# Six lower levels of the recurrent heads as products of 32 by 32 tokens in four column groups

## The reference, cut to what matters

```python
b = cumsum(logf)                                   # per channel, over the tokens
attn[t, s] = sum_k q[t, k] * k[s, k] * exp(b[t, k] - b[s, k])   for s <= t
o[t] = sum_s attn[t, s] * i[s]     # the state between chunks is the same sum over older tokens
```

## Time and profile before

| | |
|---|---|
| median of 3 runs | 1509.45 us (1509.22 to 1509.79) |
| profiled execution, first to last instruction | 1508.1 us |
| TensorE (PE) busy | 1497.7 us, 99% |
| VectorE (DVE) busy | 970.6 us, 64% |
| ScalarE (ACT) busy | 672.4 us, 45% |
| GpSimd (POOL) busy | 99.8 us, 7% |
| levels 0 to 7 of the recurrent heads | 739.2 to 823.8 us of the span |

### The profile page before, as it was taken

How to read it: one execution, slowest core, us unless ns; L and a number is a source line. 1 busy time by engine, 2 the same in 40 slices (tenths; PEclk the granted TensorE clock), 3 DMA queues, 4 the chain that set the end, 5 groups by cost and what they waited for, 6 DMA issues and landing times.

```text
span 1508.1 us, 18663 instructions
## 1 busy us (share of the span) xinstructions
PE 1497.7 (99%) x7478; PEld 1207.1 (80%) x7478; DVE 970.6 (64%) x1250; ACT 672.4 (45%) x964; POOL 99.8 (7%) x66
## 2 busy tenths in 40 slices
PE   9999999999999999999999999999999999999998
PEld 5888888778888877778888877788888888888887
DVE  5869899997895888854478367735554444432435
ACT  4656667754543667654212445522433222222232
POOL 0000001011300000023000000000210000000110
PEclk9999999999999999999999999999999999999999
DMA  9344353434684323123212342122223232322223
GB/s 392 120 154 156 115 193 122 142 112 168 221 299 178 112 87 95 53 75 114 84 57 85 102 151 84 57 84 88 108 84 112 84 112 85 112 98 84 98 98 126
DMA packets 49311, 184.70 MB, mean 122 GB/s; under 512 B 3988, under 2 KB 21012, under 8 KB 33096
## 3 DMA queue, kind: packets, MB, share of 16 engines
q1 hardware_dynamic: 32400, 174.91, 32.4%
q10 hardware_dynamic: 16824, 8.58, 2.4%
HBM read 174.98 MB, written 4.30 MB: 119 GB/s over the span
## 4 chain that ended last, share of the span: by engine, by line
PE 95%; DVE 2%; ACT 2%; issue 0%; DMA 0%; ACTq 0%; DVEq 0%
PE bank L755 25%; PE bank L757 25%; PE bank L756 25%; PE zz L1139 1%; PE bank L1094 1%; PE tt L1071 1%; PE bank L1014 1%; PE bank L1016 1%; PE bank L1015 1%; PE tt L909 1%; PE zz L1236 1%; PE zz L1082 1%; PE tt L878 1%; PE bank L1249 1%; PE zz L1083 1%; PE zz L1174 1%
## 5 line engine op out<-in xcount | busy, mean ns | idle before, releaser
L755 PE MATMUL bank<-HH,whi 128*128 128x512 f32 x1336 | 539.2, 404 | 0.4 <-DVE HL L1347 0.4
L757 PE MATMUL bank<-HH,wlo 128*128 128x512 f32 x1336 | 521.9, 391 | 0.0
L756 PE MATMUL bank<-HL,whi 128*128 128x512 f32 x1336 | 520.9, 390 | 0.0
L1395 DVE TENSOR_TENSOR wlo<-raw,whi 128x2048 fp32r<-128x2048 f32 (+1 forms) x129 | 262.8, 2039 | 91.1 <-ACT whi L2213 82.3
L755 PEld LDWEIGHTS bank<-HH,whi 128*128 128x128 f32 x1336 | 251.1, 188 | 61.7 <-issue 11.6
L757 PEld LDWEIGHTS bank<-HH,wlo 128*128 128x128 f32 x1336 | 250.8, 188 | 54.0
L756 PEld LDWEIGHTS bank<-HL,whi 128*128 128x128 f32 x1336 | 251.4, 188 | 48.9 <-issue 2.6
L2213 ACT ACTIVATE whi<-raw 128x2048 fp32r<-128x2048 f32 (+1 forms) x107 | 202.3, 1891 | 143.3 <-PE bank L757 116.9
L2885 POOL TENSOR_TENSOR SRT<-SRT 128x512 f32<-128x512 f32 x47 | 84.5, 1797 | 899.5 <-ACT SRT L2247 897.8
L757 PE MATMUL bank<-FH,wlo 128*128 128x512 f32 x176 | 68.5, 389 | 0.0
L756 PE MATMUL bank<-FL,whi 128*128 128x512 f32 x176 | 68.5, 389 | 0.0
(11 more groups left out here) (378 smaller groups left out, 2180.1 us busy)
## 6 DMA issues: line engine op xcount, KB each, us to landing
raw<-wstream SPq DMA_DIRECT2D x113, 1024.0 KB, 4.9
aslot<-tstream SPq DMA_DIRECT2D x24, 512.0 KB, 3.4
AD<-tstream SPq DMA_DIRECT2D x24, 512.0 KB, 5.5
A<-astream SPq DMA_DIRECT2D x8, 1024.0 KB, 17.9
AC<-scratch ACTq DMA_DIRECT2D x16, 512.0 KB, 5.2
QD<-QD SPq DMA_DIRECT2D x16, 256.0 KB, 3.8
raw<-wstream SPq DMA_DIRECT2D x4, 768.0 KB, 4.2
X<-xT SPq DMA_DIRECT2D x2, 1024.0 KB, 6.8
```

The costliest lines, as they stand in the source:

```text
L755: e.matmul(o, wh[:, k, c], hi[:, kb0 + k, :], start=first and k == 0, stop=False)
L756: e.matmul(o, wh[:, k, c], lo[:, kb0 + k, :], start=False, stop=False)
L757: x = e.matmul(o, wl[:, k, c], hi[:, kb0 + k, :], start=False, stop=last and k == kb - 1)
L1395: x = e.tensor_tensor(wlo[:, i % 2, c], raw[:, i % 2, c], whi[:, i % 2, c].bitcast(F32), ALU.subtract)
```

## The change

Levels 0 to 5 lie wholly inside blocks of 32 tokens, and only these blocks of the product are now made. A level is one spell: 64 matmuls of 32 by 32 tokens (4 blocks of 128, 4 heads, 4 offsets), with the output partitions, and so the column group of TensorE's array, moving with the offset from one matmul to the next. All of a level's scores fill one bank of 128 partitions by 16 groups of 32 columns. VectorE takes them with one `copy_predicated` for a level into `AD32`, which lies in the place of `OFF[0]`; level 0 has a mask of its own in the place of the product with the identity. In each level VectorE now does both halves of `grow` first and the copy after, and TensorE's spell waits for half 1 of the level before. After level 5 ScalarE writes the packed blocks to their places in `AD` with four copies of 32 partitions. `AD` and `AD32` are set to zero by GpSimd before, once the attention of the first block is done. The masks get smaller. The yields of each engine stay the same in number: 36 for the six levels on TensorE and VectorE, 48 before the first `OFF` copy on ScalarE. Counts of `s_ad` and `s_hgl` change with the number of spells.

```diff
--- before.py
+++ after.py
@@ -305,10 +305,12 @@
     HI = sbt("HI", [128, 4, 512], F32, ph2)
     GG = sbt("GG", [128, 4, S], F32, ph2)
     AD = sbt("AD", [128, 4, 4, 128], F32, ph2)
-    mk = sbt("mk", [128, 7, 128], U8, ph2)
+    mk = sbt("mk", [128, 6, 32], U8, ph2)
     OFF = [sbt("OFF", [128, 4, 128], F32, ph2)] + [
         b[:, 512 * k:512 * k + 512].rearrange("p (h t) -> p h t", h=4)
         for b, k in ((HT[0], 0), (HT[0], 1), (HT[0], 2), (HT[0], 3), (HT[1], 1))]
+    AD32 = OFF[0][:, :, :].rearrange("p h (u t) -> p (h u) t", t=32)
+    AD_all = AD[:, :, :, :].rearrange("p b h t -> p (b h) t")
     ph2.close()
     ph2 = ExitStack()
     OB = sbt("OB", [128, 2, 4, S], F32R, ph2)
@@ -1128,23 +1130,23 @@
             run(block("hf", n, "in2"))
 
         def hgrn():
-            for x in range(24):
-                lv, cs = x // 4, slice(128 * (x % 4), 128 * (x % 4) + 128)
+            for lv in range(6):
                 w.wait_ge(s_hq, 4)
                 w.wait_ge(s_hk, 4)
                 w.wait_ge(s_rr, SUM_AT["so"])
-                w.wait_ge(s_grow, grown(lv - 1, x % 4 // 2))
-                w.wait_ge(s_ad, x - 1)
-                for h in range(4):
-                    m = e.matmul(aux[x % 2][:, 128 * h:128 * h + 128], HK[:, h, cs], HQ[:, h, cs], start=True, stop=True)
+                w.wait_ge(s_grow, grown(lv - 1, 1))
+                w.wait_ge(s_ad, lv - 1)
+                for u in range(16):
+                    tb, h = divmod(u, 4)
+                    for o in (0, 32, 64, 96):
+                        ts = slice(128 * tb + o, 128 * tb + o + 32)
+                        m = e.matmul(aux[lv % 2][o:o + 32, 32 * u:32 * u + 32], HK[:, h, ts], HQ[:, h, ts], start=True, stop=True)
                 m.then_inc(s_hgl, 1)
-                yield
-                if x % 2:
-                    yield
+                yield from idle(6)
             yield
             for lv in (6, 7):
                 w.wait_ge(s_grow, grown(lv - 1, 1))
-                w.wait_ge(s_ad, 24 if lv == 6 else 26)
+                w.wait_ge(s_ad, 6 if lv == 6 else 8)
                 for tb in range(4):
                     for h in range(4):
                         for s0, t0, t1 in LEVEL_PARTS[lv]:
@@ -1157,7 +1159,7 @@
                 if f == 2:
                     yield
                 w.wait_ge(s_grow, grown(7, 1) if f < 2 else grown(8, 1))
-                w.wait_ge(s_ad, 28)
+                w.wait_ge(s_ad, 10)
                 w.wait_ge(s_off, f - 1)
                 for h in range(4):
                     m = e.matmul(aux[f % 2][:, 128 * h:128 * h + 128], HK[:, h, 128 * s:128 * s + 128],
@@ -1905,27 +1907,24 @@
                                     ALU.mult))
 
         def hgrn():
-            for x in range(24):
-                lv, tb = divmod(x, 4)
-                bv = quads(aux[x % 2][:, :])
-                w.wait_ge(s_hgl, x + 1)
-                if lv == 0:
-                    e.tensor_tensor(AD[:, tb, :, :], bv, ident.unsqueeze(1).to_broadcast([128, 4, 128]),
-                                    ALU.mult).then_inc(s_ad, 1)
-                else:
-                    w.wait_ge(s_ad, x - 3)
-                    w.wait_ge(l_mk, 16)
-                    e.copy_predicated(AD[:, tb, :, :], mk[:, lv - 1, :].unsqueeze(1).to_broadcast([128, 4, 128]),
-                                      bv).then_inc(s_ad, 1)
-                yield
-                if tb % 2:
-                    grow(lv, tb // 2)
-                    yield
+            for lv in range(6):
+                yield
+                w.wait_ge(s_hgl, lv + 1)
+                grow(lv, 0)
+                yield
+                grow(lv, 1)
+                yield
+                w.wait_ge(s_zero, 4)
+                w.wait_ge(s_ad, lv)
+                w.wait_ge(l_mk, 16)
+                e.copy_predicated(AD32, mk[:, lv, :].unsqueeze(1).to_broadcast([128, 16, 32]),
+                                  aux[lv % 2][:, :].rearrange("p (u t) -> p u t", t=32)).then_inc(s_ad, 1)
+                yield from idle(3)
             for lv in (6, 7):
                 yield from idle(1 if lv == 6 else 3)
                 for half in range(2):
-                    w.wait_ge(s_hgl, 25 if lv == 6 else 26)
-                    w.wait_ge(s_ad, 22 + 2 * half if lv == 6 else 25 + half)
+                    w.wait_ge(s_hgl, lv + 1)
+                    w.wait_ge(s_ad, 6 if lv == 6 else 7 + half)
                     for s0, t0, t1 in LEVEL_PARTS[lv]:
                         both_tb = quads(aux[half][:, :])[s0:t0, :, s0:t1].rearrange("p h (two m) -> p two h m", two=2)
                         m = e.tensor_copy(AD[s0:t0, 2 * half:2 * half + 2, :, t0:t1], both_tb)
@@ -2660,7 +2659,13 @@
             e.activation(fs, fs, ACT.Sigmoid).then_inc(s_hs, 1)
 
         def hgrn():
-            yield from idle(48)
+            yield from idle(40)
+            w.wait_ge(s_zero, 4)
+            w.wait_ge(s_ad, 6)
+            for o in (0, 32, 64, 96):
+                x = e.activation(AD_all[o:o + 32, :, o:o + 32], AD32[o:o + 32, :, :], ACT.Copy)
+            own(x)
+            yield from idle(8)
             for f in range(6):
                 if f == 2:
                     yield
@@ -2917,6 +2922,9 @@
         run(chunks)
         run(chain(out_proj(2), out_proj(3)))
 
+        w.wait_ge(s_av, 8)
+        e.memset(AD[:, :, :, :], 0.0).then_inc(s_zero, 1)
+        e.memset(OFF[0][:, :, :], 0.0).then_inc(s_zero, 1)
         for n in range(1, 8):
             for m, acc in ((2 * n - 2, R), (2 * n - 1, SQ)):
                 add(SQ_AT["so"] + m + 3, SA_AT["so"] + m + 1, T[m % 3][:, :], acc)
@@ -2969,8 +2977,9 @@
     cmask = (s <= t).astype(np.float32)
     diag = np.concatenate([np.zeros((128, 384), np.float32), ident], axis=1)
     con = np.concatenate([ident, np.ones((128, 128), np.float32), bones, cmask, diag], axis=1)
-    masks = np.stack([((s // (2 * m)) == (t // (2 * m))) & ((s // m) % 2 == 0) & ((t // m) % 2 == 1)
-                      for m in (1, 2, 4, 8, 16, 32, 64)], axis=1).astype(np.uint8).reshape(128, 896)
+    s, t = s % 32, t[:, 0:32]
+    masks = np.stack([s == t] + [((s // (2 * m)) == (t // (2 * m))) & ((s // m) % 2 == 0) & ((t // m) % 2 == 1)
+                                 for m in (1, 2, 4, 8, 16)], axis=1).astype(np.uint8).reshape(128, 192)
     return np.ascontiguousarray(con), np.ascontiguousarray(masks)
 
 
```

## The result

| | before | after |
|---|---|---|
| median, same session | 1509.53 us (1509.22 to 1509.79, 4 runs) | 1495.68 us (1495.19 to 1495.88, 4 runs) |
| ratio | | 0.9908 (95%: 0.9897 to 0.992) |
| profiled span | 1508.1 us | 1494.1 us |
| rows of TensorE in levels 0 to 5 | 192 in 24 spells | 768 in 6 spells |

A forecast was written before the change was run, and what follows sets the result against it. TensorE, busy nearly throughout, was taken to bound the kernel: 22.3 us removed and 8.4 us added give -13.9 us, so 1509.45 becomes 1495.5 us. The forecast's own range was 1494.3 to 1498, with rivals A and B 1494.3 to 1503.

The forecast's parts named there:

- TensorE bounds all, nothing swallows the gain: Whole kernel: TensorE busy 1497.7 of 1508.1 us, so time taken from it shortens the span unless a wait grows.
- Removed, 22.3 us: TensorE, levels 0 to 5: 22 ordinary spells at 0.905 us, a first at 1.07 and a late one at 1.32.
- Added, six spells at 1.40 us: TensorE, levels 0 to 5: six spells of 64 narrow matmuls over four column groups, 8.4 us in all.
- lower end: New TensorE spells: groups three and four run beside the first two, 1.335 us a spell, 8.0 us in all.
- 0.065 us: New TensorE spells: addition per spell for twice the rows to be issued in the same time.
- The page's rule: New TensorE spells: matmul starts at least about 25 ns apart, 3.2 us a spell, a time of about 1507.6 us.
- VectorE: VectorE in the levels: 24 takings-out become 6, 11 us less; no new wait, the old 0.41 us one goes.
- ScalarE and GpSimd: After level 6, four copies, 2.4 us; after the first block's attention, two clears, 4.0 us; both at cost 0.
- Rival A: New TensorE spells: no overlap beyond two column groups, 2.47 us a spell, 1501.9 us; chance 0.13.
- Rival B: VectorE's `grow` late before spells: each of five levels might lose 1 us, 1500.5 us; chance 0.07.
- Rival C: New TensorE spells: instructions come too slowly, 30 ns each, 5.2 us a spell, 1518.2 us; chance 0.04, half way 0.06.
- Rival D: Clears, copies or a wait at the end give back the levels' gain, within 0.2% of before; chance 0.03.

The follow-up runs named there:

- order runs: Changed kernel with each spell's same 64 matmuls reordered: one column group after the other, 1511.78 us; two groups at a time, 1500.84 us.
- one-group kernel: Changed kernel with each spell's 64 matmuls ordered 16 in one column group, then 16 in the next: 1511.78 us, ratio 1.0012.
- two-group kernel: Changed kernel with each spell's 64 matmuls alternating between groups 1 and 2, then 3 and 4: 1500.84 us, ratio 0.9941.
- delayed kernels: Changed kernel with extra VectorE multiplications of 448 columns ahead of `grow` in levels 1 to 5: two, 1501.96 us; four, 1507.32 us.

## Why the prediction was right

- **TensorE bounds all, nothing swallows the gain.** Right: busy time and span both fell by 14.0 us.
- **Removed, 22.3 us.** Borne out by the balance: 22.3 - 8.55 = 13.7 against a span of 14.0 less.
- **Added, six spells at 1.40 us, 8.4 in all.** 1.425 and 8.55. The lower end (1.335 us) rested on groups three and four running beside the first two, and the order runs show just that: 4.07, 2.25, 1.43 us for one, two and four groups. The value was right, its reason only in part. I took the list of a group as what sets the length: by the one-group kernel that is 31.6 ns a row, 7.9 over four groups, and the first rows of a spell do go by at 7.9. The later ones come at 8.3, and half of the columns hardly changes either: with four groups another limit, nearly as high, has taken over. The two lie so near each other that the sum can't show the difference. The 0.065 us that I added for the further rows was a guess, and that it came within 0.03 is luck. The stretch from a spell's first start to the next dense matmul, for which I gave 1.0 to 1.2 us, is 1.22.
- **The page's rule.** The Trainium skill, "TensorE: Matmul & The Clock Gate", section "Wait — 56ns, not 53.3ns?", gives some 25 ns as the nearest that two starts come. The trace doesn't agree across column groups: 8.7 ns a row here on the mean. For rows that stay in one group it doesn't contradict it: 31.6 ns.
- **VectorE.** `grow` was to be ready 1.6 to 3.5 us ahead of the spells, 1.2 ahead of level 7, 0.8 ahead of the first product between blocks. Measured are 1.5 to 3.6 (the last four spells and level 6), 1.4 and 1.1. The old wait of 0.41 us is gone. Two rows of VectorE's timeline:

```profile
780.47 0.68 DVE L1903 TENSOR_TENSOR HK<-HK,HT 128x512 f32<-128x512 f32 x1
...
789.07 0.69 DVE L1903 TENSOR_TENSOR HK<-HK,HT 128x512 f32<-128x512 f32 x1
```

These are the last multiplications of `grow` in two levels, 0.6 us each in the queue: done at 781.1 and 789.7, for spells at 783.6 and 791.2.

- **ScalarE and GpSimd.** 2.5 us against 2.4. The clears 2.3 us against 4.0 taken: the price by the column from a small clear was too high by 1.7 us, without effect.
- **Rival A** (two groups at most): the two-group kernel stands at 1500.84, where A had put the change at 1501.9; the spells of four groups, at 1.43 us, refute it. **Rival B** (VectorE late): did not occur; the delayed kernels show that the room of single levels doesn't last when every level is late: 1.3 us in each of five cost 6.3 us, more than that rival's 5, as the clock comes on top. **Rival C** (instructions too slow): its price is refuted, a further load or matmul takes 4.2 ns, not 30; whether its mechanism is what sets these 4.2 isn't shown. **Rival D**: nothing is given back.

Open: whether the 4.2 ns are the supply of instructions or the loading of weights (a kernel with the one and not the other wasn't tried), why the loads of a narrow spell start late, and the 0.3 us of the span that the spells don't account for. That much lies within what the program varies ahead of the change: the first spell starts at 739.2 before and 738.7 after, and between 738.7 and 739.8 in the other kernels.

## What to carry to other kernels

Small independent matmuls should take turns over TensorE's column groups, one after the other in program order: the same 64 took 1.43 us in turns and 4.07 group by group. They belong in one spell, as each spell of such narrow matmuls inside dense work costs about 0.37 us beside its rows; a spell of full 128 by 128 products costs 0.02, and to bundle those gains next to nothing. Beside a full TensorE, price what moves to other engines by the room that is there before the next wait, level by level, and not by their busy shares: VectorE at 64% was 1.1 to 1.5 us from being late.

## What the runs showed of the hardware that I had not expected

- Rows of 32 columns and of 16 go at one pace with four groups (1.425 and 1.405 us for 128 rows): 8.3 ns for a load and a matmul. Rows of 64 columns don't: 14 ns.
- A spell of narrow matmuls inside dense ones costs 0.37 us beside its rows: its weight loads begin only 0.31 us after the start of the last dense matmul, and the first dense ones behind it start 0.335 us apart. A spell of full products, whose loads begin ahead, costs 0.02.
- A wait of TensorE costs more than its length once it is long: after gaps of 2.65, 3.7 and 4.0 us in the delayed kernels the next four to six dense matmuls started 0.427 us apart instead of 0.228, at a granted clock near the lower level; after gaps of 0.9 to 1.05 us they didn't.
- ScalarE's copy of 32 partitions by 512 columns takes 0.63 us (2.53 for four), as long as one of 128 partitions.
